# Retention heads of a hybrid decoder step: four gate buffers, the square root behind the gate activations, the gated transposes later in the stream

## What is computed

```python
def retention_chunk(state, q, k, v, log_g):
    scores = einsum('bthd,bshd->bhts', q, k) * decay
    inner = einsum('bhts,bshe->bthe', scores, v)
    cross = einsum('bthd,bhde->bthe', q * q_decay, state)
    new_state = exp(t * log_g) * state + einsum('bshd,bshe->bhde', k * k_decay, v)
    return new_state, inner + cross

def ret_output(x, o, g, w_out):
    on = standardize(o)            # (o - mean) / sqrt(var + 1e-6), per token and head
    return x + (silu(g) * on) @ w_out
```

## Time and profile before

| | us |
|---|---|
| median of three runs | 3578.32 |
| lowest and highest | 3578.22, 3584.36 |
| profiled execution, its own time | 3580.66 |
| its span, first to last instruction | 3578.9 |
| PE busy (share of the span) | 3350.0 (94%) |
| POOL, DVE, ACT busy | 1065.0, 988.0, 959.8 |
| retention heads, about | 1319 to 2907 of the span |

### The profile page before, as it was taken

One profiled execution on the slowest core, in us unless ns is written; L12 is line 12 of the kernel. 1 busy time (PEld: TensorE's weight loads), 2 busy tenths in 40 slices (PEclk: granted clock), 3 DMA queues, 4 the chain that ended last, 5 costly groups with the idle time before them and its releaser, 6 DMA issues.

```text
span 3578.9 us, 43292 instructions
## 1 busy us (share of the span) xinstructions
PE 3350.0 (94%) x15505; PEld 2633.4 (74%) x15505; DVE 988.0 (28%) x1720; ACT 959.8 (27%) x1471; POOL 1065.0 (30%) x444
## 2 busy tenths in 40 slices
PE   6799999999998789999999999999999989999886
PEld 5687777777877678686777767686767768788765
DVE  3501244233212451313222231303132240212225
ACT  4422334233223232121312222121212131212232
POOL 5542322322332023132322223232323223333211
PEclk9999999999999899999999999999999999999988
DMA  7333221223222233333333333333333343422222
GB/s 248 107 96 97 67 68 57 66 74 119 80 82 92 87 108 101 124 115 119 120 111 107 114 118 109 119 119 121 117 115 123 119 159 130 135 72 81 77 93 84
DMA packets 211716, 380.35 MB, mean 106 GB/s; under 512 B 20448, under 2 KB 59232, under 8 KB 207520
## 3 DMA queue, kind: packets, MB, share of 16 engines
q1 hardware_dynamic: 137744, 233.34, 21.3%
q10 hardware_dynamic: 73824, 144.84, 12.1%
HBM read 318.95 MB, written 60.16 MB: 106 GB/s over the span
## 4 chain that ended last, share of the span: by engine, by line
PE 71%; DVE 8%; ACT 1%; issue 1%; DVEq 1%; ACTq 0%
PE bank L547 16%; PE bank L549 16%; PE bank L548 16%; PE bank L551 4%; PE bank L552 4%; PE bank L563 2%; DVE R L1775 2%; PE bank L880 2%; PE bank L582 2%; PE bank L871 2%; DVE R L1773 1%; PE bank L919 1%; PE bank L915 1%; PE bank L911 1%; DVEq L1510 1%
## 5 line engine op out<-in xcount | busy, mean ns | idle before, releaser
L524 POOL TENSOR_TENSOR w_lo<-w_raw,w_hi 128x1024 fp32r<-128x1024 f32 x440 | 1064.8, 2421 | 2468.5 <-ACT w_hi L977 2468.1
L547 PE MATMUL bank<-w_hi,xT_hi 128*128 128x512 f32 (+1 forms) x2880 | 1166.3, 405 | 38.4 <-ACT R L1199 17.4
L549 PE MATMUL bank<-w_hi,xT_lo 128*128 128x512 f32 (+1 forms) x2880 | 1122.9, 390 | 0.0
L548 PE MATMUL bank<-w_lo,xT_hi 128*128 128x512 f32 (+1 forms) x2880 | 1121.8, 390 | 0.0
L977 ACT ACTIVATE w_hi<-w_raw 128x1024 fp32r<-128x1024 f32 x440 | 465.5, 1059 | 1737.4 <-PE bank L552 1628.6
L547 PEld LDWEIGHTS bank<-w_hi,xT_hi 128*128 128x128 f32 x2880 | 545.4, 189 | 182.5 <-issue 29.0
L548 PEld LDWEIGHTS bank<-w_lo,xT_hi 128*128 128x128 f32 x2880 | 546.0, 190 | 115.3 <-issue 11.5
L549 PEld LDWEIGHTS bank<-w_hi,xT_lo 128*128 128x128 f32 x2880 | 544.7, 189 | 115.1
L551 PE MATMUL bank<-w_hi,xT_sample 128*128 128x512 f32 (+1 forms) x816 | 328.8, 403 | 5.4 <-DVE R L1773 4.8
L552 PE MATMUL bank<-w_lo,xT_sample 128*128 128x512 f32 (+1 forms) x816 | 316.8, 389 | 0.0
L989 ACT ACTIVATE R<-bank 128x512 f32<-128x512 f32 (+6 forms) x342 | 180.0, 532 | 399.0 <-PE bank L563 262.0
(11 more groups left out here) (172 smaller groups left out, 2270.5 us busy)
## 6 DMA issues: line engine op xcount, KB each, us to landing
w_raw<-in_w_in_ret SPq DMA_DIRECT2D x128, 512.0 KB, 3.7
w_raw<-in_w_in_even SPq DMA_DIRECT2D x80, 512.0 KB, 3.6
w_raw<-in_w_in_ret SPq DMA_DIRECT2D x128, 256.0 KB, 2.9
R<-in_state_ret ACTq DMA_DIRECT2D x64, 512.0 KB, 4.6
out_ret_state_sample<-R ACTq DMA_DIRECT2D x64, 512.0 KB, 3.1
w_raw<-in_w_out_ret SPq DMA_DIRECT2D x64, 512.0 KB, 3.6
w_raw<-in_w_out_even SPq DMA_DIRECT2D x32, 512.0 KB, 3.6
mix_scratch<-R ACTq DMA_DIRECT2D x16, 576.0 KB, 3.5
```

Of the source, the lines that this page charges most:

```text
L524: pool.tensor_tensor(wlo[:, s], raw[:, s], whi[:, s].bitcast(F32), ALU.subtract).then_inc(lo_ready, 1)
L547: pe.matmul(acc, th[:, k, tok], hi[:, kk, 0:width], start=first, stop=False)
L548: pe.matmul(acc, th[:, k, tok], lo[:, kk, 0:width], start=False, stop=False)
L549: mm = pe.matmul(acc, tl[:, k, tok], hi[:, kk, 0:width], start=False, stop=last)
```

## The change

The buffer `sg` grows from two to four tiles (one for each prompt tile). In `c_evac` the four Silus come first, each waiting only for its bank and for the product of the head before on its own buffer; then the wait for the variances and the square root; then the Silu of the sample rows. `gate_mul` takes the number of buffers. The M blocks are moved to later steps: in A from 4, 8, 12, 18, 22, 26 to 9, 13, 17, 22, 26, 30, and in `rout` from 2, 5, 8, 11, 14, 17 to 6, 9, 12, 15, 18, 21. The columns of `stat` that hold variances and roots are laid out anew (the tensor shrinks from 112 to 96 columns), with the same operations. DVE's instructions keep their order.

```diff
-RA_POINTS = [(4, "M00"), (8, "M01"), (12, "M02"), (18, "M10"), (22, "M11"), (26, "M12")]
+RA_POINTS = [(9, "M00"), (13, "M01"), (17, "M02"), (22, "M10"), (26, "M11"), (30, "M12")]
-RZ_POINTS = [(2 + 3 * n, name) for n, (_, name) in enumerate(RA_POINTS)]
+RZ_POINTS = [(6 + 3 * n, name) for n, (_, name) in enumerate(RA_POINTS)]
...
-        QK, V, ON, sg = c.take(5, CW), c.take(5, CW), c.take(5, CW), c.take(2, CW)
+        QK, V, ON, sg = c.take(5, CW), c.take(5, CW), c.take(5, CW), c.take(NT, CW)
...
             def c_evac(stage, h, i):
                 act.wait_ge(*is_full(stage, "OI", i))
                 copy(ON[0:NS, NT], bank_of(stage, "OI")[0:NS, :]).then_inc(FREE(stage, "OI"), 1)
+                for t in range(NT):
+                    act.wait_ge(*is_full(stage, ("C", t), i))
+                    act.wait_ge(gated, 5 * (1 + h) + (t + 1))
+                    act.activation(sg[:, t], bank_of(stage, ("C", t))[:, :], ACT.Silu).then_inc(FREE(stage, ("C", t)), 1)
                 act.wait_ge(var_ready, plan.st["gn"] + 1 + h)
-                act.activation(stat[:, 101:106], stat[:, 96:101], ACT.Sqrt).then_inc(std_ready, 1)
-                gate_evac(stage, "C", i, 2 + h, sg, sgs)
+                act.activation(stat[:, 74:79], stat[:, 51:56], ACT.Sqrt).then_inc(std_ready, 1)
+                act.wait_ge(*is_drained(stage, ("C", NT), i))
+                act.activation(sgs[0:NS, :], sgs[0:NS, :], ACT.Silu).then_inc(sil_ready, 1)
...
-            def gate_mul(stage, tag, i, n, L, dst, buf, sbuf):
+            def gate_mul(stage, tag, i, n, L, dst, buf, sbuf, bufs=2):
...
-                    do(v.tensor_tensor(d, d, buf[:, t % 2], ALU.mult).then_inc(gated, 1))
+                    do(v.tensor_tensor(d, d, buf[:, t % bufs], ALU.mult).then_inc(gated, 1))
...
-                gate_mul(stage, "C", i, 2 + h, Lin(L.c + GPC, L.k, L.i), lambda t: ON[0:rows(t), t], sg, sgs)
+                gate_mul(stage, "C", i, 2 + h, Lin(L.c + GPC, L.k, L.i), lambda t: ON[0:rows(t), t], sg, sgs, NT)
```

More of the change, by code:

```diff
@@ L288, in build @@
         cst = sb("cst", [P, NCONST])
-        stat = sb("stat", [P, 112])
+        stat = sb("stat", [P, 96])
         bn = sb("bn", [P, 12])
@@ L1908, in group_stats @@
                 do(v.bn_stats(bn[0:r, 0:6], ON[0:r, c]))
-                do(v.bn_aggr(stat[0:r, 48 + 2 * c:50 + 2 * c], bn[0:r, 0:6]))
+                do(v.bn_aggr(stat[0:r, 64 + 2 * c:66 + 2 * c], bn[0:r, 0:6]))
             def group_norm(h):
                 own, sam = bass.ds(h, 1), bass.ds(h + RH, 1)
-                do(v.tensor_scalar(stat[:, 96:100], stat[:, 49:57:2], qd2[:, own], EPS, ALU.mult, ALU.add))
-                do(v.tensor_scalar(stat[0:NS, 100:101], stat[0:NS, 57:58], qd2[0:NS, sam], EPS, ALU.mult, ALU.add).then_inc(var_ready, 1))
+                do(v.tensor_scalar(stat[:, 51:55], stat[:, 65:73:2], qd2[:, own], EPS, ALU.mult, ALU.add))
+                do(v.tensor_scalar(stat[0:NS, 55:56], stat[0:NS, 73:74], qd2[0:NS, sam], EPS, ALU.mult, ALU.add).then_inc(var_ready, 1))
                 v.wait_ge(std_ready, plan.st["gn"] + 1 + h)
-                newton(stat[:, 106:111], stat[:, 96:101], stat[:, 101:106], stat[:, 58:63])
-                do(v.tensor_scalar(stat[:, 106:110], stat[:, 106:110], qd[:, own], None, ALU.mult))
-                do(v.tensor_scalar(stat[0:NS, 110:111], stat[0:NS, 110:111], qd[0:NS, sam], None, ALU.mult))
+                newton(stat[:, 80:85], stat[:, 51:56], stat[:, 74:79], stat[:, 56:61])
+                do(v.tensor_scalar(stat[:, 80:84], stat[:, 80:84], qd[:, own], None, ALU.mult))
+                do(v.tensor_scalar(stat[0:NS, 84:85], stat[0:NS, 84:85], qd[0:NS, sam], None, ALU.mult))
                 for c in ALL:
                     r = rows(c)
-                    do(v.tensor_scalar(ON[0:r, c], ON[0:r, c], stat[0:r, 48 + 2 * c:49 + 2 * c], stat[0:r, 106 + c:107 + c],
+                    do(v.tensor_scalar(ON[0:r, c], ON[0:r, c], stat[0:r, 64 + 2 * c:65 + 2 * c], stat[0:r, 80 + c:81 + c],
                                        ALU.subtract, ALU.mult))
```

## The result

The changed kernel takes **3620.11 us** (median of 4 runs, 3617.44 to 3622.95) against 3580.52 us for the kernel before (4 runs, 3578.22 to 3584.36): ratio 1.011, 95% interval 1.0092 to 1.0127. It is slower, by 1.1%.

The account below looks back on a forecast made before the run. The chain root, Newton step, normalisation, products, sample sum, which frees bank 4, was taken as the bound. 7 x (3.1 + 0.44 + 2.2) = 40.2, plus 2.0 for the last head, on 3578.3 gives 3620.5 us; range 3603 to 3631.

Parts of the forecast that it names:

- What sets the end of the piece: Retention heads: root, Newton step, normalisation, products, sample sum free bank 4 and set the end; gate bank stalls are slack.
- The root 3.1 us later: Looped heads: four Silus and a table load ahead of the root delay it and DVE's whole chain by 3.1 us.
- 0.86: Upper bound for Silu spacing on ACT; 0.54 us was taken, 0.86 us would bring the root 1.0 us later still.
- The table loads: ACT: 1.28 us per load without extra drain; three per looped head instead of two, the third costing nothing.
- The rival of slower loads: Each of the two loads ahead of the root takes as much again: 17.9 us on top, 3638 us, chance 0.04.
- M00, +0.44: Transpose block moved from step 4, inside the bank 4 wait, to step 9 in a full stream: +0.44 us per head.
- The clock, +2.2: PE at half clock after the new 6.8 us stall: +2.2 us per head, bounds nothing and 2.4.
- The sum for a looped head: Root delay 3.1, moved M00 0.44 and slow clock 2.2 us added, in each of seven heads.
- The last head, +2.0,: Sample tile starts 0.6 us earlier after 9.9 us idle, but M00 +0.44 and half clock +2.2 follow: together +2.0.
- The reload of x: Last head: ends 5.5 us later, making DVE about 3 us late; costed at nothing, 3 us as upper end.
- The rival "bank 4 does not decide": PE need not wait for the sample sum, so gate bank waits and last head's slow clock go: 3551 us, chance 0.04.

Follow-up runs that it names:

- Experiment 1: The changed kernel with the square root put back ahead of the four Silus, four buffers and late M blocks kept: 3593.2 us, ratio to before 1.0034.
- experiment 4: The changed kernel with DVE's sample sum moved from behind the products to right behind the variances, before the wait for the root: 3564.87 us, ratio 0.9955.
- experiment 2: The changed kernel with the M blocks at their old steps, four buffers and late root kept: 3615.97 us, ratio 1.0099.
- Experiment 3: The changed kernel with 28 unused 512-column matmuls added before the sample tile of each looped head: 3606.72 us, ratio 1.0068.
- experiment 7: Experiment 4 with M00 at step 10, the projection's blocks one step later, and two split_mix instead of five before the last head's norm: 3548.99 us.
- experiment 9: Experiment 4 with one wait more: ACT holds the next weight split until DVE's fourth product is done: 3552.86 us, ratio 0.9925.
- experiment 10: Experiment 7 with the added ACT wait of experiment 9: 3548.17 us, ratio 0.9909.

## Why the prediction was right, and where its sizes were off

It forecast 42.2 us more than before. The medians are 39.6 apart, the profiled executions 39.9. That the number 3620.5 lies 0.4 us from the measured median is partly luck: the median of before came out 2.2 us higher with a fourth run, and the terms were off in both directions (looped heads 1.8 us too low, last head 0.8 too high, and 3.2 us came back outside the heads, where nothing was forecast).

- **What sets the end of the piece** was right: L1564 releases the sample tile in all eight heads, the waits at the gate banks were slack and their 25.1 us bought nothing. Experiment 1 puts the root back and two thirds of the loss are gone; experiment 4 frees the bank early and all of it is.
- **The root 3.1 us later:** between the end of gemm C and the sample tile there were 9.19 us, now 12.15: +2.96. The Silus stood 0.5 us apart, not 0.86.
- **The table loads:** 1.28 us each, neighbours within 0.03 us, the third one hidden in ACT's 8.86 us of waiting. The rival of slower loads is out.
- **M00, +0.44:** experiment 2 gives 0.69 for the steps together, with another pattern of stalls and clock, so M00 alone was not measured.
- **The clock, +2.2:** right in kind, undersized. Experiment 3 gives 2.48. Twelve matmuls at 0.43 in place of 0.23 us are 2.4, and the first one is slow besides.
- **The sum for a looped head**, 5.74, is 6.00.
- **The last head, +2.0,** is +1.2. The sample tile starts at 2965.34 behind 9.83 us of idle time, where I had said 9.9. The clock term was too large here: the slow stretch behind the stall was shorter than in a looped head (0.68 on average over 5.15 us, against 0.50). The reload of x was late by the few microseconds that I had named, DVE waits for it until 3013.77, and PE does not wait.
- **Not in the prediction:** the 4.3 us that come back behind the heads, and 1.1 us before them. The prediction took unchanged code to cost the same. In the twelve profiled executions it does so only within 5.3 us behind the heads (444.4 to 449.7) and 6.6 us before them (the last reciprocal ahead of the heads, L1515 in the kernel before, starts between 1292.3 and 1298.9). Effects of a few microseconds are therefore read from the head period here, not from one whole time.
- **The rival "bank 4 does not decide"** (3551 us, chance 0.04) was wrong for this change but right as a mechanism: experiments 4, 7, 9 and 10 make it true in the looped heads, and then the four buffers and the later steps pay.

One thing that I had as sure in the first experiment was wrong: that only idle times of the length in the earlier trace rows lower the clock.

## What to carry to other kernels

Before a stall is removed, find what the same engine waits for next and whether it was there in time by chance: here a wait of 0.3 us at most named the instruction that set the time, and 25.1 us of waits elsewhere were slack. Two more buffers paid only when the instruction that frees the last bank was moved up into idle time as well; each of the two alone made the kernel slower, by 40 and by 33 us, and together they made it faster. When an edit makes one engine earlier, look at what starts earlier with it and what that will collide with.

## What the hardware showed that was not expected

- **The clock falls behind shorter gaps than the rows of the kernel before show.** Idle times of 0.81 and 1.65 us with 3 us of matmuls between them left it at 1.00. Idle times of 0.83 and 2.50 us with 5.6 us of matmuls between them brought 0.50 behind the second in five heads of seven (experiment 1), one of 2.09 us brought slow matmuls in the last head of experiment 10, and one of 6.54 us brought 0.50 in all seven heads of the changed kernel.
- **A gap filled with matmuls that nobody needs gave 13.4 us** (experiment 3). What the stall of 6.54 us costs at this place is its length and 2.5 us more.
- **DVE stands still in some of its instructions while POOL subtracts.** In all 40 normalisations of the changed kernel a single one takes 0.54 to 0.55 us; in experiment 4 the longest takes 2.56:

```profile
L1930 DVE TENSOR_SCALAR R<-R,stat x40: 537/548/2556, 1520.7 to 2907.3; 128x512 f32<-128x512 f32 x32, 64x512 f32<-64x512 f32 x8
```

It is about the length of a POOL subtraction, 2.39 us, which the smallest instruction shows best: in experiment 10 a DVE instruction of 128x128 that takes 0.28 us takes 2.48 beside POOL:

```profile
2897.79 0.28 DVE L1965 TENSOR_TENSOR xT_sample<-xT_sample 128x128 fp32r<-128x128 f32 x1
...
2901.32 2.48 DVE L1965 TENSOR_TENSOR xT_sample<-xT_sample 128x128 fp32r<-128x128 f32 x1
```

```profile
2897.86 5.78 POOL L524 TENSOR_TENSOR w_lo<-w_raw,w_hi 128x1024 fp32r<-128x1024 f32 x2 [2.60 <-ACT w_hi L977]
```

If the two shared a rate, both instructions would be slower by the same factor; they are slower by 4.7 and by 8.9. So DVE does not run at half speed but waits for the other's instruction to end. Not every DVE instruction is held, though. At one place of the changed kernel a POOL subtraction meets both kinds:

```profile
916.72 2.46 POOL L524 TENSOR_TENSOR w_lo<-w_raw,w_hi 128x1024 fp32r<-128x1024 f32 x1 [3.94 <-ACT w_hi L977]
917.18 0.69 DVE L1778 TENSOR_TENSOR R<-bank,R 128x512 f32 x1 [0.25 <-issue]
918.04 1.70 DVE L1780 TENSOR_TENSOR R<-R  x1 [0.17 <-issue]
```

L1778, which reads a PSUM bank and R, takes 0.69 us beside POOL as without it, in all 26 cases that lie wholly inside a subtraction. L1780 reads SBUF alone: it takes 0.68 to 0.69 us with POOL idle, and its 28 instructions that start inside a subtraction take 1.65 to 2.40 us; the one shown ends 0.56 us behind POOL.

The Trainium skill, page "SBUF — State Buffer", section "SBUF: two separate sides", describes it so: the port pair that the two engines share is an exclusive lock for the whole instruction, and the other one fully blocks. By its rule the DVE instruction must be one in a 2-port mode, or one with two SBUF inputs against a GpSimd instruction that reads SBUF. The rows of L1778 and L1780 agree with this. In which mode the normalisations ran, a tensor_scalar of float32, was not measured here, but they were blocked.
